# A decoder trunk of two layers: earlier first gathers, VectorE operations that signal themselves, and phase ends copied out by halves

## The chip, the cores and the metric

One core of a Trainium2 chip runs the whole program. The metric is the device time of one execution in microseconds.

## The reference

The input x is 256 positions of 1024 numbers in float32. Two residual layers follow; each is a mixer and then a mixture of single-neuron experts. The mixer of layer 0 is pooling with dilated attention, the one of layer 1 a Mamba-2 scan. The expert part, which moves most of the bytes, is this for each block of 128 positions:

```python
def block(xb):
    q = jnp.einsum('nd,de->ne', xb, w_q).astype(jnp.float32).reshape(n, PEER_HEADS, 2, PEER_HALF)
    s = jnp.einsum('nhie,ike->nhik', q, keys)
    top_s, top_i = lax.top_k(s, PEER_TOPK)
    ...
    best_s, best_pos = lax.top_k(cand_s, PEER_TOPK)
    idx = jnp.take_along_axis(cand_i, best_pos, axis=-1)
    gate = jax.nn.softmax(best_s, axis=-1)
    u = expert_u[idx]
    act = jax.nn.gelu(jnp.einsum('nhkd,nd->nhk', u, xb, preferred_element_type=jnp.float32), approximate=False)
    coef = (gate * act).astype(xb.dtype)
    return jnp.einsum('nhk,nhkd->nd', coef, expert_v[idx])
```

There are 8 heads, and each picks 16 of 16384 experts for every position. So every position fetches 128 rows of u and 128 rows of v for each layer.

## The kernel before

The program has four **phases**: layer 0 with block 0, layer 0 with block 1, layer 1 with block 0, layer 1 with block 1. A phase has 128 **slots**, 16 for each head. One slot is one gather of 128 partitions by 2048 numbers (u and v of one expert for each position), 1 MB. `gather` on GpSimd (POOL, L500) issues them into `ring`, which has 12 places, in pairs: a pair goes out once TensorE has summed the pair that used the same places (`pairs_summed0` and `pairs_summed1`). The first gather of each head also waits for that head's expert numbers (`idx_ready`). The ring's places serve as weight buffers at first (`staged`): gathers 0 to 11 also wait for `staged_free`, which PE tells when it has used a weight chunk. Gathers 8 and 9 wait for the query chunk of heads 4 and 5, gathers 10 and 11 for the one of heads 6 and 7.

For each slot VectorE (DVE) takes a dot product (`dot`, L1584). For each pair ScalarE (ACT) takes the gelu (L1141), DVE multiplies by the gates (`coefficients`, L1592), ACT makes two diagonal matrices (L1148), and PE adds both rows into four accumulator banks `acc` in PSUM (`sum_pair`, L928, 16 records for a pair). Even slots are summed in one half of the partitions of a bank, odd slots in the other half, crossed over.

Beside this stream, the mixer and the queries of the next phase run in small pieces. Each engine's program is written by generators (`Side`), and tables of numbers (`KNOTS`, `TOPS_DUE`, `ROUTE_DUE`) say before which slot each piece is put. `queries` on PE makes a head's query (L610), ACT copies it (L990), PE multiplies it with the keys (L890), ACT copies the scores, DVE picks the 16 largest of both halves (`tops`, L1483 to L1487). `route` then works in three parts on DVE: part 0 adds up the candidates and picks the 16 best, part 1 (`expert_numbers`, L1533 to L1552) computes the expert numbers, part 2 the gates. `queries` also makes the norm's gain on all partitions with 8 products (16 records, L899), behind the first head's keys. DVE needs it for `hn` later on.

In the very first phase nothing runs beside: the mixer of block 0 and the queries of all heads come ahead of the first slots (`T_EARLY`, `T_ROUTED`).

At a **phase end** ACT copies the odd sums from `acc` to `odd_sums` (`copy_odd`, L1160). DVE waits for all of it and adds the even sums from `acc` on top, into `h` (`read_acc`, L1604, behind slot 2). PE waits for that, then puts the new phase's own stream into `acc` (`take_stream`, L912, 4 products, 8 records), and only then sums the new phase's first pair. Part 1 of `route` for head 1 stands right behind `read_acc` on DVE.

At the **start** SP issues x, then the constants (312 KB), then the first weight chunk in two halves of 1024 KB, then more chunks. PE begins with transposes of x, for which it needs the identity, a part of the constants.

Many steps end with `lane.tell(name)`: DVE waits for its own last operation and then adds to a semaphore with an instruction of its own. `lane(instruction, name)` lets the operation itself add to that semaphore.

## Time and profile before

| | us |
|---|---|
| median of 3 runs | 1625.21 (1623.24 to 1626.09) |
| the profiled execution | 1629.12 |
| its span, first to last instruction | 1627.3 |
| PE busy | 1202.7 (74%) |
| DVE busy | 1171.0 (72%) |
| POOL busy | 600.7 (37%) |
| ACT busy | 527.0 (32%) |
| bytes moved | 665.05 MB, mean 409 GB/s |

The page cuts the span in 40 slices and gives for each the GB/s that the 16 DMA engines moved. The view by windows gives the same for stretches of one's own choice. In the timeline, a bracket behind an instruction tells how long its engine stood idle before it, and what ended that. "DVEq" and "ACTq" are the instruction queues of DVE and ACT, where semaphores are added to.

### The profile page before, as it was taken

How to read it: one execution, taken by the hardware profiler on the slowest of the kernel's cores; microseconds unless marked ns; L12 is line 12 of the kernel's file. 1: busy time of each engine (PE TensorE's matmuls, PEld its weight loads, DVE VectorE, ACT ScalarE, POOL GpSimd, SP SyncE). 2: the span in 40 equal slices, each digit the busy share in tenths (PEclk: the TensorE clock that was granted, in tenths of full speed). 3: DMA queues.
4: the chain of work that ended last, by engine and by line, in shares of the span. 5: the costliest groups of instructions: out<-in, count | busy, mean ns of one | idle time of the engine just before them, and what ended most of it. 6: DMA issues, size and time to landing. Idle time of an engine off the chain costs nothing.

```text
span 1627.3 us, 21833 instructions
## 1 busy us (share of the span) xinstructions
PE 1202.7 (74%) x7488; PEld 591.0 (36%) x7488; DVE 1171.0 (72%) x3339; ACT 527.0 (32%) x1231; POOL 600.7 (37%) x542
## 2 busy tenths in 40 slices
PE   8876786868748887978687788799697855555565
PEld 3661232225415663533264355444234611111111
DVE  4479768668768687786677866788956886666665
ACT  0222143222224564642132355455311232222221
POOL 1034433533334244233333323441433345444442
PEclk9998897989879998998898799999798988777767
DMA  9879999999999999999999999999999989999997
GB/s 380 339 297 412 423 421 421 422 421 421 421 417 415 423 425 420 420 423 422 422 422 422 384 424 424 421 421 417 395 414 424 416 354 421 422 421 421 421 421 315
DMA packets 84079, 665.05 MB, mean 409 GB/s; under 512 B 9376, under 2 KB 9392, under 8 KB 11008
## 3 DMA queue, kind: packets, MB, share of 16 engines
q0 software_dynamic: 74752, 540.13, 80.3%
q1 hardware_dynamic: 9216, 123.53, 18.0%
q8 instruction: 59, 0.97, 0.2%
q14 instruction: 52, 0.43, 0.1%
HBM read 662.57 MB, written 1.05 MB: 408 GB/s over the span
## 4 chain that ended last, share of the span: by engine, by line
DMA 29%; PE 29%; DVE 26%; ACT 7%; issue 7%; POOL 2%; another core or an unknown queue 0%; DVEq 0%; POOLq 0%; ACTq 0%; SPq 0%
DMA ring<-in_experts,idx 28%; PE acc L928 11%; DVE ring L1584 9%; PE act_bank L610 7%; PE dve_bank L596 6%; DVE h L1390 2%; DVE onehot L1219 2%; DVE scratch L1219 2%; POOL ring L500 2%; ACT diag L1148 1%; ACT L990 1%; ACT h L1070 1%; PE act_bank L596 1%; ACT scratch L990 1%; PE act_bank L890 1%
## 5 line engine op out<-in xcount | busy, mean ns | idle before, releaser
L500 POOL DMA_INDIRECT ring<-in_experts,idx x510 | 573.5, 1125 | 947.6 <-PE acc L928 732.0
L928 PE MATMUL acc<-ring,diag 64*64 64x512 f32 x4080 | 608.2, 720 | 315.8 <-ACT diag L1148 307.9
L1584 DVE CUSTOM_DVE_ANT_0 ring<-ring,hn 128x1024 f32<-128x1024 f32 x512 | 620.7, 1224 | 220.1 <-DMA ring<-in_experts,idx 197.1
L928 PEld LDWEIGHTS acc<-ring,diag 64*64 64x64 f32 x4080 | 155.1, 153 | 665.2 <-ACT diag L1148 427.2
L1141 ACT ACTIVATE acts<-dots 128x2 f32<-128x2 f32 x256 | 52.1, 203 | 674.6 <-DVE dots L1584 642.2
L610 PE MATMUL act_bank<-hnT,wbuf 128*128 128x128 f32 x1728 | 218.0, 284 | 23.3 <-ACT h L1070 19.5
L1148 ACT ACTIVATE diag<-cst,coefs 128x64 f32<-128x64 f32 x512 | 150.3, 340 | 252.1 <-DVE coefs L1592 215.4
L610 PEld LDWEIGHTS act_bank<-hnT,wbuf 128*128 128x128 f32 x1728 | 205.2, 197 | 70.1 <-issue 63.0
L990 ACT ACT_TABLE_LOAD x80 | 102.6, 1283 | 19.4 <-DMA rowc<-in_rows 17.0
L1592 DVE TENSOR_TENSOR coefs<-acts,gate 128x2 f32<-128x2 f32 x256 | 42.7, 167 | 79.5 <-ACT acts L1141 64.7
L1141 ACT ACT_TABLE_LOAD x68 | 87.2, 1283 | 6.2 <-DVE dots L1584 0.3
L1390 DVE SCALAR_TENSOR_TENSOR h<-scratch,colc,h 128x128 f32<-128x128 f32 x192 | 64.7, 406 | 0.8
L596 PE MATMUL dve_bank<-wbuf,scratch 128*128 128x512 f32 x128 | 63.2, 627 | 0.3 <-PE dve_bank L596 0.2
L990 ACT ACTIVATE scratch<-act_bank 128x512 f32<-128x512 f32 (+3 forms) x73 | 35.3, 484 | 74.9 <-PE act_bank L610 51.7
L837 PE MATMUL act_bank<-wbuf,hnT 128*128 128x512 f32 x128 | 59.0, 598 | 0.0
L890 PE MATMUL act_bank<-keysT,scratch 128*128 128x128 f32 x128 | 23.3, 307 | 34.6 <-issue 19.7
L1584 DVE DVE_READ_ACCUMULATOR2_ANT dots<- 128x1 f32 x512 | 42.2, 82 | 0.0
L596 PEld LDWEIGHTS dve_bank<-wbuf,scratch 128*128 128x128 f32 x128 | 23.4, 198 | 42.6 <-issue 42.6
L596 PE MATMUL dve_bank<-wbuf,hnT 128*128 128x512 f32 x64 | 33.9, 675 | 5.2 <-DVE hnT L1219 3.3
L890 PEld LDWEIGHTS act_bank<-keysT,scratch 128*128 128x128 f32 x128 | 17.7, 200 | 45.1 <-issue 45.1
L837 PEld LDWEIGHTS act_bank<-wbuf,hnT 128*128 128x128 f32 x128 | 23.3, 190 | 24.7 <-issue 24.3
L1483 DVE MAX8 top_s<-scores 128x8 f32<-128x128 f32 x64 | 15.5, 284 | 22.8 <-ACTq L361 22.5
(173 smaller groups left out, 1024.8 us busy)
## 6 DMA issues: line engine op xcount, KB each, us to landing
wbuf<-in_weights SPq DMA_DIRECT2D x48, 2048.0 KB
ring<-in_weights SPq DMA_DIRECT2D x7, 2048.0 KB, 19.4
ring<-in_experts,idx POOLq DMA_INDIRECT x510
kept<-in_weights SPq DMA_DIRECT2D x2, 2048.0 KB, 21.8
wbuf<-in_weights SPq DMA_DIRECT2D x2, 1024.0 KB, 7.0
scratch<-in_bias POOLq DMA_DIRECT2D x1, 1024.0 KB, 12.0
scratch<-in_bands POOLq DMA_DIRECT2D x1, 768.0 KB, 13.3
h<-in_x SPq DMA_DIRECT2D x1, 512.0 KB, 3.7
```

The source lines that it names most:

```text
L500: pool.indirect_dma_start(ring[:, n % RING], None, io[f"experts{layer}"], bass.IndirectOffsetOnAxis(idx[:, at:at + 1], 0),).then_inc(sem(f ...
L596: ins = pe.matmul(out[:, 0:cols], lhsT[:, k], w[:, k], start=first and k == tiles[0], stop=last and k == tiles[-1])
L610: ins = pe.matmul(out[:, n * P:(n + 1) * P], w[:, k, j * P:(j + 1) * P], hnT[:, k], start=k == 0, stop=k == KD - 1)
L837: ins = pe.matmul(out_z, hnT[:, k], w[:, k], start=k == 0, stop=k == KD - 1)
L890: ins = pe.matmul(out[:, i * NK:(i + 1) * NK], qT[:, 2 * hd + i], keysT[:, layer, i], start=True, stop=True)
L928: last[rows] = pe.matmul(acc[rows][half][home:home + HALF_P], diag[part, n % DIAGS], ring[part, slot, D + half * CW:D + (half + 1) * CW], ...
L990: lane(act.activation(out, in_, func, **more), name)
L1141: act.activation(acts[:, cols], dots[:, cols], ACT.Gelu).then_inc(sem("gelu_done"), 1)
L1148: ins = act.activation(diag[:, (q * GROUP + s) % DIAGS], folded, ACT.Copy, scale=coefs[:, q * GROUP + s:q * GROUP + s + 1])
L1219: lane(dve.tensor_tensor(out, in0, in1, op), name)
L1390: done = lane.start(dve.scalar_tensor_tensor(out, tiles[:, j, tap:tap + P], taps[:, t, tap:tap + 1], out, ALU.mult, ALU.add))
L1584: dve.tensor_tensor_reduce(out=ring[:, slot, 0:D], in0=ring[:, slot, 0:D], in1=hn[:, phase % NBLK], scale=1.0, scalar=0.0, op0=ALU.mult, o ...
```

## The change

- **Start.** The constants are sorted anew, and SP first issues only 160 of their 624 columns (identity and the mixer's gains, 80 KB), then x, then the first half chunk as two quarters of 512 KB, the second half, and the other 464 columns. PE waits for a quarter, and for the second quarter behind its second product.
- **First head.** In the first phase, head 0 has its expert numbers in two halves: as soon as the 8 best are picked, DVE computes their 8 numbers and signals `first_idx_ready`, on which gather 0 waits. The other 8 follow. ACT takes the exponential of head 0 behind the second head's scores instead of the third's. Heads 2 and later have their tops one piece later.
- **Gain.** The 8 products of the gain stand ahead of the first head's query in all four phases.
- **Signals.** Some 20 places with `lane.tell` on DVE now let the last operation signal (those of `mixer0`, `mixer1`, `prepare`, `tops`, `route`).
- **Phase ends.** DVE copies the even sums from `acc` into `h` (`copy_even`) without waiting for ACT; both signal each half (512 columns). PE starts the first pair's sums in a half when it is copied out. `take_stream` stands behind the fourth pair, and adds to what is there. DVE adds the odd sums behind slot 3 (`add_odd`). Part 1 of head 1 goes out at slot 4 or later.

The core of the diff (most places of the signals are left out):

```diff
-EARLY_HEADS, ROUTED_HEADS = 6, 3
+EARLY_HEADS, ROUTED_HEADS = 6, 2
...
+TAKEN_AT = 3 * GROUP + 1
...
+ROUTE_FROM = 4
...
-            ROUTE_DUE.append(max(_due, _part) if _head else _due)
-TOPS_FIRST = 3
-TOPS_DUE = [-3, -2, -2, 0, 1, 1, 3, 5]
+            if _head == 1:
+                _due = max(_due, _phase * SLOTS + ROUTE_FROM + _part - 1) if _phase and _part else max(_due, _part)
+            ROUTE_DUE.append(_due)
+TOPS_FIRST = 2
+TOPS_DUE = [-3, -2, 0, 1, 2, 3, 4, 5]
...
-C_ID, C_TRI, C_STRI, C_IOTA = 0, P, 2 * P, 3 * P
+C_ID, C_GAIN = 0, P
+C_FFN = C_GAIN + DEPTH * KD
+C_FIRST = C_TRI = C_FFN + DEPTH * KD
+C_STRI = C_TRI + P
+C_IOTA = C_STRI + P
...
-C_GAIN = C_FOLD + HALF_P
-C_FFN = C_GAIN + DEPTH * KD
-C_ROWS = C_FFN + DEPTH * KD
+C_ROWS = C_FOLD + HALF_P
...
+            sp.dma_start(cst[:, 0:C_FIRST], io["consts"][:, 0:C_FIRST]).then_inc(sem("first_consts_loaded"), 16)
...
-            sp.dma_start(cst, io["consts"]).then_inc(sem("consts_loaded"), 16)
...
-                            sp.dma_start(flat[:, 0:CH // 2], w[:, 0:CH // 2]).then_inc(sem("half_chunk_in"), 16)
+                            quarter, half = slice(0, CH // 4), slice(CH // 4, CH // 2)
+                            sp.dma_start(flat[:, quarter], w[:, quarter]).then_inc(sem("quarter_chunk_in"), 16)
+                            sp.dma_start(flat[:, half], w[:, half]).then_inc(sem("half_chunk_in"), 16)
...
+                            sp.dma_start(cst[:, C_FIRST:], io["consts"][:, C_FIRST:]).then_inc(sem("consts_loaded"), 16)
...
-                if n % TOPK == 0:
+                if n == 0:
+                    pool.wait_ge(sem("first_idx_ready"), 1)
+                elif n == TOPK // 2 or n % TOPK == 0:
...
                 if chunks[0] == 1:
-                    pe.wait_ge(sem("half_chunk_in"), 16)
+                    pe.wait_ge(sem("quarter_chunk_in"), 16)
                     return wbuf[:, 0]
...
                     score(groups[1])
+                def second_quarter():
+                    if b == 0:
+                        pe.wait_ge(sem("half_chunk_in"), 16)
...
-                                                  halfway={0: other_half, 3: first_scores}.get(c))
+                                                  between={0: {1: second_quarter, 3: other_half},
+                                                           3: {3: first_scores}}.get(c, {}))
...
+                pe.wait_ge(sem("consts_loaded"), 16)
+                for half in range(2):
+                    out = fill("dve")
+                    for j in range(4):
+                        row = layer * KD + 4 * half + j
+                        ins = pe.matmul(out[:, j * P:(j + 1) * P], ident[:, row:row + 1].to_broadcast([P, P]),
+                                        gain_rows, start=True, stop=True)
+                    ins.then_inc(sem("dve_full"), 1)
...
-                    if hd == 0:
-                        yield at + 3
-                        for half in range(2):
-                            out = fill("dve")
-                            for j in range(4):
-                                row = layer * KD + 4 * half + j
-                                ins = pe.matmul(out[:, j * P:(j + 1) * P], ident[:, row:row + 1].to_broadcast([P, P]),
-                                                gain_rows, start=True, stop=True)
-                            ins.then_inc(sem("dve_full"), 1)
...
                                         h[part, phase % NBLK, half * CW:(half + 1) * CW],
-                                        start=True, stop=False, skip_group_check=True)
+                                        start=False, stop=False, skip_group_check=True)
                     ins.then_inc(sem("stream_taken"), 1)
...
+                    if start and g:
+                        pe.wait_ge(sem("even_copied"), 2 * (g // STEPS - 1) + half + 1)
+                        pe.wait_ge(sem("odd_copied"), 2 * (g // STEPS - 1) + half + 1)
...
-                                                   start=start and odd == 1, stop=stop, skip_group_check=True)
+                                                   start=start, stop=stop, skip_group_check=True)
...
-                    if n == GROUP:
-                        if phase:
-                            pe.wait_ge(sem("acc_read"), phase)
-                            pe.wait_ge(sem("odd_copied"), phase)
-                        take_stream(phase)
...
+                    if n == TAKEN_AT:
+                        take_stream(phase)
...
-            pe.wait_ge(sem("consts_loaded"), 16)
+            pe.wait_ge(sem("first_consts_loaded"), 16)
...
-                lane.after(started)
-                lane.tell("odd_copied")
+                    lane.after(started)
+                    lane.tell("odd_copied")
...
-                        started[n] = lane.start(step(*row))
+                        last = step == steps[-1] and n == len(rows) - 1
+                        started[n] = lane.start(ops[step](*row), name if last else None)
...
-                lane(dve.tensor_copy(norm_root, stat[:, 32:33]))
-                lane.tell("root_ready")
+                lane(dve.tensor_copy(norm_root, stat[:, 32:33]), "root_ready")
...
-                                 top_i[:, hd, i * TOPK:(i + 1) * TOPK]) for i in range(2)))
-                        lane.tell("scores_taken")
+                                 top_i[:, hd, i * TOPK:(i + 1) * TOPK]) for i in range(2)), name="scores_taken")
...
-                    top16((cand, best, best_pos))
-                def expert_numbers(hd):
-                    row, place, beyond = (pos_f[:, n * TOPK:(n + 1) * TOPK] for n in range(3))
+                def expert_numbers(hd, lo, hi, name):
+                    picks = slice(lo, hi)
+                    row, place, beyond = (pos_f[:, n * TOPK:(n + 1) * TOPK][:, picks] for n in range(3))
...
-                    started = [lane.start(dve.tensor_scalar(pos_hi, best_pos, 4, None, ALU.logical_shift_right)),
-                               lane.start(dve.tensor_scalar(pos_lo, best_pos, 15, None, ALU.bitwise_and)),
-                               lane.start(dve.tensor_copy(top_if, top_i[:, hd]))]
+                    started = [lane.start(dve.tensor_scalar(pos_hi[:, picks], best_pos[:, picks], 4, None,
+                                                            ALU.logical_shift_right)),
+                               lane.start(dve.tensor_scalar(pos_lo[:, picks], best_pos[:, picks], 15, None,
+                                                            ALU.bitwise_and))]
+                    if lo == 0:
+                        started.append(lane.start(dve.tensor_copy(top_if, top_i[:, hd])))
...
-                    lane.start(dve.tensor_copy(row, pos_hi))
+                    lane.start(dve.tensor_copy(row, pos_hi[:, picks]))
...
-                    lane(dve.tensor_copy(place, pos_lo))
+                    lane(dve.tensor_copy(place, pos_lo[:, picks]))
...
-                    hot = onehot.rearrange("p (i s a) -> p i s a", i=2, s=TOPK)
-                    flat = onehot.rearrange("p (n a) -> p n a", a=TOPK)
-                    tt(flat, pos_f[:, 0:2 * TOPK].unsqueeze(2).to_broadcast([P, 2 * TOPK, TOPK]),
-                       iota16.unsqueeze(1).to_broadcast([P, 2 * TOPK, TOPK]), ALU.is_equal)
-                    tt(hot, hot, key.unsqueeze(2).to_broadcast([P, 2, TOPK, TOPK]))
-                    lane(dve.reduce_sum(picked, flat, AX))
-                    stt(row, picked[:, 0:TOPK], float(NK), picked[:, TOPK:], ALU.mult, ALU.add)
-                    at = b * SLOTS + hd * TOPK
-                    lane(dve.tensor_copy(idx[:, at:at + TOPK], row))
-                    lane.tell("idx_ready")
+                    n = hi - lo
+                    hot = onehot.rearrange("p (i s a) -> p i s a", i=2, s=TOPK)[:, :, picks]
+                    found = picked.rearrange("p (i s) -> p i s", i=2)[:, :, picks]
+                    both = pos_f[:, 0:2 * TOPK].rearrange("p (i s) -> p i s", i=2)[:, :, picks]
+                    tt(hot, both.unsqueeze(3).to_broadcast([P, 2, n, TOPK]),
+                       iota16.unsqueeze(1).unsqueeze(1).to_broadcast([P, 2, n, TOPK]), ALU.is_equal)
+                    tt(hot, hot, key.unsqueeze(2).to_broadcast([P, 2, n, TOPK]))
+                    lane(dve.reduce_sum(found, hot, AX))
+                    stt(row, found[:, 0], float(NK), found[:, 1], ALU.mult, ALU.add)
+                    at = b * SLOTS + hd * TOPK + lo
+                    lane(dve.tensor_copy(idx[:, at:at + n], row), name)
...
-                        lane(dve.tensor_copy(last_idx, place[:, 0:2 * GROUP]))
-                        lane.tell("last_idx_ready")
+                        lane(dve.tensor_copy(last_idx, place[:, 0:2 * GROUP]), "last_idx_ready")
...
-                ts(expd, best, best[:, 0:1], None, ALU.subtract)
-                lane.tell("best_ready")
+                start = 0
+                if layer == b == hd == 0:
+                    top16((cand, best, best_pos), steps=range(2))
+                    start = TOPK // 2
+                    expert_numbers(hd, 0, start, "first_idx_ready")
+                    top16((cand, best, best_pos), steps=range(2, 5))
+                else:
+                    top16((cand, best, best_pos))
+                ts(expd, best, best[:, 0:1], None, ALU.subtract, name="best_ready")
...
-                expert_numbers(hd)
+                expert_numbers(hd, start, TOPK, "idx_ready")
...
-            def read_acc(phase):
+            def copy_even(phase):
...
-                lane.need("odd_copied")
...
-                        started = lane.start(dve.tensor_tensor(h[part, phase % NBLK, cols], odd_sums[part, cols],
-                                                               acc[rows][half][part], ALU.add))
-                lane.after(started)
-                lane.tell("acc_read")
+                        started = lane.start(dve.tensor_copy(h[part, phase % NBLK, cols], acc[rows][half][part]))
+                    lane.after(started)
+                    lane.tell("even_copied")
+            def add_odd(phase):
+                for half in range(2):
+                    lane.need("odd_copied")
+                tt(h[:, phase % NBLK], h[:, phase % NBLK], odd_sums, ALU.add)
...
-                        read_acc(phase - 1)
+                        copy_even(phase - 1)
+                    if n == GROUP + 1 and phase:
+                        add_odd(phase - 1)
...
             tops_side.upto(0)
+            dve.wait_ge(sem("consts_loaded"), 16)
             routes.upto(ROUTE_PARTS - 1)
```

**PE, first phase, from the transposes of h behind the mixer to the second head's query** (L610 is a query, L890 the keys, L899 the gain). Before:

```order
L618 MATMUL act_bank<-cst,h 128x128 x8
L610 MATMUL act_bank<-hnT,ring 128x128 x16
L890 MATMUL act_bank<-keysT,scratch 128x128 x2
L899 MATMUL dve_bank<-cst 128x128 x8
L610 MATMUL act_bank<-hnT,ring 128x128 x16
```

Now, where L621 is a query, L915 the keys and L893 the gain:

```order
L629 MATMUL act_bank<-cst,h 128x128 x8
L893 MATMUL dve_bank<-cst 128x128 x8
L621 MATMUL act_bank<-hnT,ring 128x128 x16
L915 MATMUL act_bank<-keysT,scratch 128x128 x2
L621 MATMUL act_bank<-hnT,ring 128x128 x16
```

The gain moved ahead of the first query, into the place where PE waits for ACT's copies of `hnT`.

**DVE, first phase, the first head from the places of its 8 best** (`best_pos`, first row). Before:

```order
L1484 MAX_INDEX best_pos<-best,cand 128x8
L1485 MATCH_REPLACE cand<-best,cand 128x136
L1486 MAX best<-cand 128x8
L1487 MAX_INDEX best_pos<-best,cand 128x8
L1223 TENSOR_SCALAR expd<-best 128x16
L1533 TENSOR_SCALAR pos_hi<-best_pos 128x16
L1534 TENSOR_SCALAR pos_lo<-best_pos 128x16
L1535 CAST top_if<-top_i 128x32
L1537 CAST pos_f<-pos_hi 128x16
L1539 CAST pos_f<-pos_lo 128x16
L1226 SCALAR_TENSOR_TENSOR pos_f<-pos_f 128x16
L1542 TENSOR_TENSOR pos_f<-pos_f 128x16
```

Now, from the ninth row behind that same `MAX_INDEX` (L1492) on:

```order
L1235 TENSOR_TENSOR onehot<-pos_f,cst 128x2x128
L1235 TENSOR_TENSOR onehot<-onehot,top_if 128x2x128
L1561 TENSOR_REDUCE picked<-onehot 128x2x8
L1242 SCALAR_TENSOR_TENSOR pos_f<-picked 128x8
L1564 CAST idx<-pos_f 128x8
L1493 MATCH_REPLACE cand<-best,cand 128x136
L1494 MAX best<-cand 128x8
L1495 MAX_INDEX best_pos<-best,cand 128x8
L1239 TENSOR_SCALAR expd<-best 128x16
L1540 TENSOR_SCALAR pos_hi<-best_pos 128x8
```

Eight expert numbers (`idx`) are now written ahead of the second half of the picking, on arrays half as long.

**DVE, end of the first phase, from the second slot of the new phase on** ("ISA ring,dots" and "ISA dots" are one dot product). Before:

```order
L1592 TENSOR_TENSOR coefs<-acts,gate 128x2
L1584 ISA ring,dots<-ring,hn 128x1024
L1584 ISA dots 128x1
L1604 TENSOR_TENSOR h<-scratch,acc 64x512 x4
L1533 TENSOR_SCALAR pos_hi<-best_pos 128x16
L1534 TENSOR_SCALAR pos_lo<-best_pos 128x16
L1535 CAST top_if<-top_i 128x32
```

Now:

```order
L1609 TENSOR_TENSOR coefs<-acts,gate 128x2
L1601 ISA ring,dots<-ring,hn 128x1024
L1601 ISA dots 128x1
L1620 COPY h<-acc 64x512 x4
L1601 ISA ring,dots<-ring,hn 128x1024
L1601 ISA dots 128x1
L1235 TENSOR_TENSOR h<-h,scratch 128x1024
L1609 TENSOR_TENSOR coefs<-acts,gate 128x2
L1601 ISA ring,dots<-ring,hn 128x1024
L1601 ISA dots 128x1
```

Four copies took the place of four additions, one addition of 1024 columns was added behind the next dot product, and the 13 operations of part 1 of head 1 went behind slot 4.

## Rows read from the trace of the kernel before

**Rows 1.** The page's GB/s in 40 slices, and its group of the dot products

```profile
GB/s 380 339 297 412 423 421 421 422 421 421 421 417 415 423 425 420 420 423 422 422 422 422 384 424 424 421 421 417 395 414 424 416 354 421 422 421 421 421 421 315
...
L1584 DVE CUSTOM_DVE_ANT_0 ring<-ring,hn 128x1024 f32<-128x1024 f32 x512 | 620.7, 1224 | 220.1 <-DMA ring<-in_experts,idx 197.1
```

**Rows 2.** By windows: stretch, length, busy time of PE, PEld, DVE, ACT, POOL

```profile
core 0: us, PE busy (x) PEld busy (x) DVE busy (x) ACT busy (x) POOL busy (x), PEclk, DMA share, GB/s
70.00:80.00 10.00, 9.12 (x72) 8.77 (x71) 4.63 (x27) 1.11 (x3) 0.00 (x0) 0.91 0.30 128
80.00:90.00 10.00, 8.51 (x72) 8.19 (x72) 6.67 (x27) 1.67 (x5) 3.86 (x4) 1.00 0.33 111
110.00:120.00 10.00, 7.34 (x53) 4.12 (x51) 7.81 (x35) 4.37 (x8) 2.82 (x4) 1.00 0.56 204
900.00:930.00 30.00, 23.56 (x160) 10.33 (x156) 25.40 (x65) 9.20 (x24) 12.78 (x12) 0.81 0.95 371
1320.00:1330.00 10.00, 7.29 (x60) 2.00 (x55) 9.06 (x23) 2.37 (x9) 5.02 (x5) 0.95 0.48 177
```

**Rows 3.** Timeline of the first 10 us, PE and DVE: start, us, instruction

```profile
5.27 1.97 PE L618 MATMUL dve_bank<-cst,h 128*128 128x128 f32 x8 [5.27 <-DMA cst<-in_consts]
8.79 9.57 PE L596 MATMUL dve_bank<-wbuf,hnT 128*128 128x512 f32 x16 [1.55 <-DMA wbuf<-in_weights]
...
6.52 1.51 DVE L1219 TENSOR_TENSOR hnT<-dve_bank,cst 128x512 f32<-128x512 f32 x2 [0.68 <-PE dve_bank L618]
```

**Rows 4.** The chain of work that ended last, until 120 us: start, us, what

```profile
18.65 7.12 PE dve_bank L596 x16
...
74.35 1.79 PE dve_bank L899 x16
76.14 3.59 PE act_bank L610 x32
...
89.26 2.96 another core or an unknown queue
...
110.93 1.87 PE acc L912 x8
```

**Rows 5.** Timeline of PE, the first head's query

```profile
67.61 5.47 PE L610 MATMUL act_bank<-hnT,ring 128*128 128x128 f32 x32 [1.84 <-ACT hnT L1110]
```

**Rows 6.** Timeline of DVE, the first head's numbers

```profile
78.49 0.29 DVE L1484 FIND_INDEX8 best_pos<-best,cand 128x8 uint32<-128x136 f32 x1
...
79.96 0.23 DVE L1223 TENSOR_SCALAR expd<-best 128x16 f32<-128x16 f32 x1
80.34 0.18 DVE L1533 TENSOR_SCALAR pos_hi<-best_pos 128x16 uint32<-128x16 uint32 x1
...
81.37 0.69 DVE L1219 TENSOR_TENSOR onehot<-pos_f,cst 128x512 f32<-128x512 f32 x1
...
83.75 0.17 DVE L1552 CAST idx<-pos_f 128x16 uint32<-128x16 f32 x1
```

**Rows 7.** Timeline of POOL, gathers 0 and 10

```profile
84.95 1.01 POOL L500 DMA_INDIRECT ring<-in_experts,idx  x1 [29.58 <-DVEq L361]
...
115.88 0.94 POOL L500 DMA_INDIRECT ring<-in_experts,idx  x1 [9.41 <-PEq L586]
```

**Rows 8.** Groups by form, DVE: two that stand nearest to new ones

```profile
L1219 DVE TENSOR_TENSOR scratch<-scratch,hn 128x256 f32<-128x256 f32 x8 | 3.4, 425 | 0.3
...
L1219 DVE TENSOR_TENSOR h<-scratch 128x1024 f32<-128x1024 f32 x1 | 1.2, 1226 | 0.0
```

**Rows 9.** Timeline, ends of phase 2 (1312) and of phase 1 (896)

```profile
1311.94 2.44 ACT L1160 ACTIVATE scratch<-acc 64x512 f32<-64x512 f32 x4
1314.55 2.83 DVE L1604 TENSOR_TENSOR h<-scratch,acc 64x512 f32<-64x512 f32 x4 [2.12 <-ACTq L361]
...
1319.28 1.12 PE L928 MATMUL acc<-ring,diag 64*64 64x512 f32 x2
...
1323.76 1.25 POOL L500 DMA_INDIRECT ring<-in_experts,idx  x1 [11.99 <-PE acc L928]
...
896.20 2.83 DVE L1604 TENSOR_TENSOR h<-scratch,acc 64x512 f32<-64x512 f32 x4 [1.22 <-ACTq L361]
```

More of the change, by code:

```diff
@@ L591, in chunk_used, with row_products @@
                 chunk_free()
-            def row_products(out, lhsT, w, first=True, last=True, cols=CW, tick=None, halfway=None, tiles=range(KD)):
+            def row_products(out, lhsT, w, first=True, last=True, cols=CW, tick=None, between={}, tiles=range(KD)):
                 for k in tiles:
@@ L1477, in mixer1, with top16 @@
                     lane.tell("h_ready")
-            def top16(*rows):
-                steps = [
+            def top16(*rows, steps=range(5), name=None):
+                ops = [
                     lambda src, values, places: dve.max(values[:, 0:8], src),
```

52 lines of the change are left out of this document (22 added, 30 removed).

## The prediction

> **What bounds the kernel now.** I read the page's GB/s by slices first. Almost everywhere the transfers run at 421 to 424 GB/s, and DVE's dot products, the nearest engine work, stood idle 220.1 us, of it 197.1 for gathers [rows 1]. So the stream of gathers sets the pace, and a microsecond is won only where the stream stands still: 665.05 MB at 422 GB/s are 1576 us of a span of 1627.3, and the other 51 us are holes. The view by windows prices each hole as (422 − its rate) / 422 × its length [rows 2]: 70 to 80 us 7.0 us, 80 to 90 us 7.4, 110 to 120 us 5.2, the end of phase 1 (900 to 930) 3.6, the end of phase 2 (1320 to 1330) 5.8. The end of phase 0 shows only in the slices of 417 and 415, (5 + 7) / 422 × 40.7 = 1.2 us [rows 1]. The change works on all of these. The chain of waits then tells what ends each hole: at the start PE's products, the first query, the first head's numbers; at a phase end the copies out of `acc` and the first pair's sum behind them.
>
> **Start.** PE waits for the constants until 5.27, and before the first chunk's products 1.55 us for the half chunk; their other operand `hnT` is done at 6.52 + 1.51 = 8.03 [rows 3]. Now 232 KB of constants and 512 KB of weights come behind what PE needs first. That is 0.75 MB, 1.8 us at 422 GB/s. But `hnT` allows only 8.79 − 8.03 = 0.76, and it can itself move by some tenths since its constants are 80 KB instead of 312. Against this, x is now the second DMA in SP's queue and one more 512 KB DMA is issued. I also see PE at its lower clock level in this stretch: 16 products take 9.57 us, the next 16 take 7.12 [rows 3, 4]; the 2.45 could come back in part if PE starts otherwise. I take **0.6 us**, the near end; bounds −0.3 (one issue of x late) and +2.2 (all of it).
>
> **Signals.** Behind `expd` (79.96 + 0.23 = 80.19) the next operation starts at 80.34, 0.15 us later, where neighbours without a `tell` follow in some hundredths [rows 6]. So a `tell` costs DVE about 0.1. Four or five lie on the way to the first gather: **0.4 us**. The hundred others lie beside DVE's waits and are worth nothing.
>
> **Gain ahead of the first query.** PE idles 1.84 us before that query, waiting for ACT's copies of `hnT`, and then needs 5.47 us for 32 records; the next 32 take 3.59, and the granted clock of that stretch is 0.91 against 1.00 after it [rows 2, 4, 5]. The 16 records of the gain take 1.79 us [rows 4] and fill just this idle time. If the clock then stays at its full level, the query takes 3.59: **1.9 us** for head 0 (bounds 0 and 1.9). For PE's later queries the 1.79 that stood between heads 0 and 1 vanish too.
>
> **Half numbers.** Before: 8 places at 78.49 + 0.29 = 78.78, `idx` at 83.75 + 0.17 = 83.92 [rows 6], gather 0 at 84.95 [rows 7]. From `pos_hi` on the chain takes 83.92 − 80.34 = 3.58. In halves, the second picking, `expd` and the `tell` fall out of the way (80.34 − 78.78 = 1.56), and the three operations on `onehot` have 256 columns: 0.43 for 0.69, 3 × 0.26 = 0.8 [rows 6, 8]. Together **2.4 us**. Head 0 pays for them with 12 more small operations, about 2 us of DVE, behind the signal. The second half is needed by gather 8 only, some ten microseconds later at 1.24 us a gather. POOL has nothing else queued there.
>
> Gather 0 thus goes out 0.6 + 0.4 + 1.9 + 2.4 = 5.3 us earlier, at about **79.6**.
>
> **The second hole.** Gather 10 waits 9.41 us for PE, to 115.88 [rows 7]: PE must be through with the last query's weights. On this path DVE's numbers don't lie. What does: start 0.6, signals 0.4, clock 1.9, the gain's 1.8, and `take_stream`, 1.87 us at 110.93 [rows 4], which goes behind the fourth pair. Sum 6.6, gather 10 at about 109.3. What lies behind it moves by that, so **the head is worth 6.6 us**, of which 5.3 came already by gather 0. Bounds: 3.8 (start −0.3, clock 0) and 8.2 (start 2.2).
>
> **Phase ends.** At the end of phase 2 ACT copies to 1314.38, DVE has waited 2.12 us for it, adds for 2.83 to 1317.38; then come `take_stream` and at 1319.28 the first pair; the gather goes out at 1323.76 after 11.99 us idle of POOL [rows 9]. Now DVE starts at once, at 1314.55 − 2.12 = 1312.43, and PE can sum half 0 when 2 of the 4 copies are made. At 0.7 us each (2.83 / 4) that is 1313.9, and 1315.2 for both halves. From the first pair's start to the gather it took 1323.76 − 1319.28 = 4.5: begun at 1313.9 it gives 1318.4, and I take 1318.5, **5.2 us earlier**, half 1 being ready while half 0 is summed. Of the hole's 5.8 I take 5.4 (bounds 4 and 5.8); its rest is the time that the row of gathers needs to build up. The end of phase 1 is another matter: DVE waited only 1.22 [rows 9], and the new addition of 1024 columns gives 1.23 back before the second pair. The hole there (3.6) comes from DVE's other work in slots 2 to 6, which now lies a little later. I take 0.6 (bounds 0 and 3.6), and for phase 0's end 0.5 (0 and 1.2). Together **6.5 us**, bounds 4 and 10.6.
>
> `take_stream` behind the fourth pair costs PE the same as before; `sum_pair` carries two waits more, which are met. Three additions of 1.23 us [rows 8] and the 12 small operations are about 5 us more of DVE: hidden by its waits for gathers, 197.1 us [rows 1]; without that cover they would cost those 5 us.
>
> The new addition reads two SBUF arrays beside POOL's gather issues, and POOL's issue at a phase end already takes 1.25 us against 0.94 at gather 10 [rows 7, 9]. If one blocks the other for its whole length, each of three additions costs 1.2 us: 3.7 less. The Trainium skill (SBUF — State Buffer, Who interferes with whom) says that a DVE instruction with two SBUF inputs and a GpSimd one that uses SBUF share a port pair under an exclusive lock. By it the gain would be 9.4 us, not 13.1. I don't take this off, since twelve gathers are in flight and the row shows 0.3 us at most.
>
> **Sum.** 6.6 + 6.5 = 13.1 us. The profiled execution took 1629.12, so 1616.0 for it; it was 3.9 above the median, 1625.21, and against that the forecast is **1612**.
>
> **Rivals.** (A) As forecast, both bounds sum to 7.8 and 18.8; the likely part is 9 to 17 us, 1608 to 1616. Chance 0.55. (B) More: the start brings its 2.2 and the ends of phases 0 and 1 close as well; 17 to 20, 1605 to 1608. For it the queue behind `hnT`; against it that DVE, not the copies, is late at those ends. 0.15. (C) Less: the clock stays low in the first query (−1.9), and the stall of 2.96 us at 89.26, which the chain gives to an unknown queue just as the first gathers land [rows 4], comes 5 us sooner and hits PE's queries or DVE's numbers of the second half; with the lock above 13.1 − 1.9 − 3 − 2 = 6, so 1616 to 1620. For it: the stall is in the trace, and it has no cause in the program. 0.20. (D) No gain: the earlier gathers only wait elsewhere, since from gather 12 on places come free by DVE's dots, PE's pairs and their diagonals; the head's 6.6 is given back where DVE is 7.8 of 10 us busy and catches up [rows 2], and the ends keep about 2: 1623. Against it the 421 GB/s just behind. 0.07. (E) Slower, by one mechanism: DVE is the bound wherever the stream falls behind. Then the holes are DVE's backlog, no release helps, and the 5 us of new DVE work at the three ends and the first head come on top: 1630. It decides from the point where DVE's share right behind a hole is at 10 of 10; it is 9.06 of 10 in 1320 to 1330 [rows 2]. Against it: in that window POOL had stood 11.99 us for PE's sum, not for a dot. 0.03. That the change doesn't do what it says has no room of its own: the order shows each move.
>
> **Numbers.** 0.2% is 3.3 us, about what a measurement of this kernel can tell from no change: faster is below 1622.0, slower above 1628.5. A, B, C and a part of D lie below: 0.91 faster, 0.06 same, 0.03 slower. The range takes A, most of B and all of C: 1604 to 1620.
>
> **What would show it.** Right: the constants' wait ends before 5.2; the first query takes about 3.6 with next to no idle before it; the first `idx` is written near 78.6 and gather 0 is issued near 79.6; gather 10 near 109; POOL's idle at the end of phase 2 falls from 12 to about 7, and the window 1320 to 1330 is back at about 420 GB/s. Four copies of about 0.7 and an addition of 1.2 stand at each phase end. Wrong in its steps: a first query still at 5.5 (clock); gather 0 at 79.6 but gather 10 still beyond 113 (another thing than PE's order releases it); gathers earlier but a new hole between 90 and 110 us (case C or D); DVE without idle time and additions longer than 1.3 us at the ends (lock, case E).

## The result, and the profile after

| | before | changed |
|---|---|---|
| median of 20 runs | 1625.22 us (1623.24 to 1627.21) | 1627.29 us (1625.16 to 1628.93) |
| ratio, 95% interval | | 1.0013 [1.0007, 1.0019] |
| profiled execution | 1629.12 | 1627.79 |
| its span | 1627.3 | 1625.8 |

The change costs some 2 us. I had forecast 1612 within 1604 to 1620, and the measured time lies above all of that. Most single steps did happen, though. Timelines of the changed kernel, of PE, DVE and POOL:

```profile
5.40 1.94 PE L629 MATMUL dve_bank<-cst,h 128*128 128x128 f32 x8 [5.40 <-DMA h<-in_x]
8.19 8.90 PE L607 MATMUL dve_bank<-wbuf,hnT 128*128 128x512 f32 x16 [0.85 <-DVE hnT L1235]
...
66.47 3.84 PE L621 MATMUL act_bank<-hnT,ring 128*128 128x128 f32 x32
...
78.56 0.17 DVE L1564 CAST idx<-pos_f 128x8 uint32<-128x8 f32 x1
...
79.70 1.02 POOL L511 DMA_INDIRECT ring<-in_experts,idx  x1 [25.57 <-DVE idx L1564]
...
105.70 1.32 POOL L511 DMA_INDIRECT ring<-in_experts,idx  x1 [7.57 <-PEq L597]
...
120.22 0.94 POOL L511 DMA_INDIRECT ring<-in_experts,idx  x1 [9.16 <-PE acc L947]
```

The first query takes 3.84 us and not 5.47 [rows 5], the first half of the numbers is there at 78.56, gather 0 goes out at 79.70 for 84.95 and gather 10 at 105.70 for 115.88 [rows 7]. But then POOL stands 9.16 us for a pair's sum, until gather 14 at 120.22. The view by windows (columns as in [rows 2]):

```profile
80.00:90.00 10.00, 8.49 (x72) 8.19 (x72) 9.47 (x42) 1.93 (x5) 7.87 (x8) 1.00 0.86 322
110.00:120.00 10.00, 3.69 (x16) 0.80 (x16) 6.09 (x30) 4.25 (x8) 0.94 (x1) 0.54 0.91 352
120.00:130.00 10.00, 6.35 (x36) 2.25 (x38) 9.32 (x32) 2.17 (x9) 3.26 (x4) 0.61 0.60 214
900.00:930.00 30.00, 21.58 (x155) 10.18 (x151) 24.77 (x75) 10.08 (x24) 12.72 (x13) 0.84 0.95 371
1300.00:1320.00 20.00, 9.90 (x52) 2.42 (x56) 18.77 (x55) 7.94 (x18) 9.17 (x8) 0.72 0.99 392
1320.00:1330.00 10.00, 9.68 (x72) 3.98 (x64) 7.21 (x16) 2.38 (x9) 4.55 (x5) 0.87 0.99 376
```

Against [rows 2] two things are to be seen. The hole of 204 GB/s at 110 to 120 is not gone, it is now one of 214 at 120 to 130. And the hole of 177 at 1320 to 1330 is nearly closed (376), yet the end did not come sooner. The page's GB/s by slices says the same:

```profile
GB/s 377 343 364 375 422 422 421 422 421 421 422 422 405 422 424 420 422 423 423 422 422 423 384 424 423 421 421 423 399 425 421 420 394 422 421 421 421 421 421 242
```

The last slice has 242 for 315 [rows 1]: most bytes are through some microseconds earlier, and the kernel waits at its end for something else. The same at the end of the changed kernel, by windows:

```profile
1600.00:1605.00 5.00, 1.95 (x16) 0.51 (x16) 2.62 (x5) 0.83 (x4) 0.00 (x0) 1.00 1.01 409
1605.00:1610.00 5.00, 3.01 (x16) 0.62 (x16) 2.63 (x5) 0.80 (x4) 0.00 (x0) 0.58 0.41 166
1610.00:1615.00 5.00, 3.75 (x20) 0.85 (x20) 3.36 (x6) 0.79 (x3) 0.00 (x0) 0.50 0.07 27
```

From 1610 to 1615 the DMA share is 0.07 and the rate 27 GB/s: a sixteenth of 1.01 and of 421 is 0.063 and 26. One of 16 DMA engines is at work, and the dot products wait for it:

```profile
1607.71 1.22 DVE L1601 CUSTOM_DVE_ANT_0 ring<-ring,hn 128x1024 f32<-128x1024 f32 x1 [1.23 <-DMA ring<-in_experts,idx]
...
1612.60 1.23 DVE L1601 CUSTOM_DVE_ANT_0 ring<-ring,hn 128x1024 f32<-128x1024 f32 x1 [1.25 <-DMA ring<-in_experts,idx]
```

The trace also has the time of each of the 16 additions to a gather's semaphore. The Trainium skill (DMA: Bandwidth & Descriptors, Why a DMA increments its semaphore by 16 and not by 1) says that each engine posts its own and that they finish independently. The trace agrees: in the changed kernel they spread over 0.5 to 1.8 us at 125 to 140 us and over 11.0 us at the end, where 15 of the 16 lie within 1.5 us.

**Theory 1** (slow engine): one DMA engine falls behind the other 15, and the end hangs on it. It catches up while the stream stands still. So a hole is free up to its lag, and closing one gains nothing. **Theory 2** (order): at the head DVE's and ACT's fixed order sets when places come free, and the tops, put one piece later, spoil it. The rival to both: the new parts themselves cost what they save.

### The profile page after: what moved, and what is told of

Same layout as the page of the kernel before. It is cut to its first block, busy times and chain, and to the rows that moved or that the text cites. A ratio compares the mean times of both kernels' runs of the same rounds, so it can differ in the third digit from the quotient of the medians.

```text
span 1625.8 us, 21843 instructions
## 1 busy us (share of the span) xinstructions
PE 1202.8 (74%) x7488; PEld 589.3 (36%) x7488; DVE 1174.8 (72%) x3354; ACT 527.1 (32%) x1231; POOL 600.7 (37%) x542
## 4 chain that ended last, share of the span: by engine, by line
DMA 30%; DVE 27%; PE 27%; ACT 8%; issue 6%; POOL 1%; SPq 0%; ACTq 0%; POOLq 0%; DVEq 0%
DMA ring<-in_experts,idx 30%; PE acc L947 12%; DVE ring L1601 9%; PE act_bank L621 5%; PE dve_bank L607 4%; DVE h L1399 2%; DVE onehot L1235 2%; ACT L1006 2%; ACT diag L1165 2%; PE act_bank L854 1%; ACT h L1086 1%; PE act_bank L607 1%; DVE scratch L1235 1%; POOL ring L511 1%; ACT scratch L1006 1%
## 5 line engine op out<-in xcount | busy, mean ns | idle before, releaser
L947 PE MATMUL acc<-ring,diag 64*64 64x512 f32 x4080 | 616.2, 730 | 348.8 <-ACT diag L1165 329.2
L621 PE MATMUL act_bank<-hnT,wbuf 128*128 128x128 f32 x1728 | 215.0, 282 | 20.7 <-ACT h L1086 19.3
L621 PEld LDWEIGHTS act_bank<-hnT,wbuf 128*128 128x128 f32 x1728 | 202.2, 195 | 68.4 <-issue 66.2
L915 PE MATMUL act_bank<-keysT,scratch 128*128 128x128 f32 x128 | 22.8, 302 | 29.8 <-issue 18.4
L915 PEld LDWEIGHTS act_bank<-keysT,scratch 128*128 128x128 f32 x128 | 17.2, 195 | 41.5 <-issue 41.5
L1491 DVE MAX8 top_s<-scores 128x8 f32<-128x128 f32 x64 | 15.5, 283 | 20.5 <-ACTq L367 20.4
```

The source lines that it names most:

```text
L621: ins = pe.matmul(out[:, n * P:(n + 1) * P], w[:, k, j * P:(j + 1) * P], hnT[:, k], start=k == 0, stop=k == KD - 1)
L947: last[rows] = pe.matmul(acc[rows][half][home:home + HALF_P], diag[part, n % DIAGS], ring[part, slot, D + half * CW:D + (half + 1) * CW], ...
```

## The experiments

Each was timed beside the kernel before, apart from the first. Where a time is set against one that was not timed together with it, the kernel before stood within 1624.9 to 1626.2 beside all of them, so such a difference is good to about 1 us. In the expectations "tops" are the steps L1491 to L1495 that pick the 16 largest scores, and "dot n" is DVE's dot product for slot n in the first phase. One slip of mine stands in them: what the expectations of tops_back, whole_numbers, gain_back and tops_later call dot 8, at 122.9 us in the changed kernel, is dot 6 (and the dots 4 and 6 of tops_later are dots 2 and 4); the text here counts rightly.

**The kernel before again.**

> The kernel before once more, for a second profile: the first one (1629.12 us) lies above all 20 of its timed runs (1623.2 to 1627.2). Slow-engine theory: the transfers of one gather are done by 16 DMA engines, and one of them falls behind the others; in the first profile the 16 landings of a gather spread over 8 us shortly ahead of the end of phase 2, and over 1.6 us behind the hole of 1320 to 1330, in which the late engine caught up. The second profile shows the same: a spread of 7 to 13 us at 1290, under 3 us at 1350, and a hole of 177 GB/s or so in 1320 to 1330. Rival (the spread in the first profile was chance, all engines alike): a spread under 3 us throughout. Time 1624 to 1627 by both.

1624.67 us. The spread was 7.9 us at 1290 and 1.6 at 1350, as theory 1 has it. But the hole was not one of 177 GB/s in 1320 to 1330, as expected; it lay across both windows:

```profile
1300.00:1320.00 20.00, 9.06 (x48) 2.60 (x52) 15.90 (x51) 7.32 (x15) 6.14 (x5) 0.74 0.81 337
1320.00:1330.00 10.00, 7.05 (x60) 1.69 (x52) 9.09 (x22) 2.76 (x11) 7.69 (x7) 1.00 0.88 338
```

That is 85/422 × 20 + 84/422 × 10 = 6.0 us, and the late engine lost none of it. Two gathers on either side of the hole have half of their landings 9.7 us apart (at 1315.1 and 1324.8), but their last ones, at 1323.0 and 1325.5, only 2.5 us apart, as in the full stream. More important is the head. Here gather 0 goes out at 83.89 and gather 10 at 110.47, 5.4 us earlier than in the trace on which I had forecast:

```profile
83.89 1.01 POOL L500 DMA_INDIRECT ring<-in_experts,idx  x1 [29.58 <-DVEq L361]
...
110.47 0.94 POOL L500 DMA_INDIRECT ring<-in_experts,idx  x1 [8.86 <-PEq L586]
```

Beside this one, the changed kernel leads by 5.1 us at dot 0 (87.98 for 93.07) and is 2.4 behind at dot 6 (122.90 for 120.54). It is 2.8 behind at dot 62 and 1.1 at the last dot of the phase.

**Phase ends taken back, and phase ends alone.** In `ends_back` the diff's parts on the phase ends are undone in the changed kernel; in `ends_only` they alone are made in the kernel before. The core of the latter's edit (the halves, the copies and part 1 of head 1 are left out):

```diff
-                    if n == GROUP:
-                        if phase:
-                            pe.wait_ge(sem("acc_read"), phase)
-                            pe.wait_ge(sem("odd_copied"), phase)
-                        take_stream(phase)
...
+                    if n == TAKEN_AT:
+                        take_stream(phase)
...
+                    if n == GROUP + 1 and phase:
+                        add_odd(phase - 1)
```

> The changed kernel (1627.3 us) with the phase ends of before: read_acc waits for all odd copies and adds, take_stream ahead of the first pair, part 1 of head 1 not held back. Slow-engine theory: the hole at the end of phase 2 lets the late engine catch up and costs it nothing, so the time stays within 1.5 us of the changed kernel, 1625.8 to 1628.8, though the slice at 1320 falls back below 250 GB/s; the landings of the last gathers then spread over less than 5 us instead of 11. Rival (the new phase ends do save their 4 to 6 us, and the head loses more than it gains): 1631 to 1633.

> The kernel before (1625.2 us) with the new phase ends alone (even copies without waiting, halves, take_stream behind the fourth pair, add_odd, part 1 of head 1 from slot 4). Slow-engine theory: the hole at 1320 to 1330 closes (over 350 GB/s for 177), the landings of the last gathers spread over 8 to 12 us, and the time stays within 1.5 us of before: 1623.7 to 1626.7. Rival (all engines alike, the hole was worth its 5.8 us): 1619 to 1621. Third (the new ends cost what the changed kernel lost): 1627 to 1629.

`ends_back`: 1626.68, 0.6 below the changed kernel (ratio to before 1.0004 [0.9995, 1.0013], where the changed kernel has 1.0013). `ends_only`: 1625.77 beside 1625.92 for before, ratio 1.0003 [0.9994, 1.0012]. Both times are theory 1's. The sizes in the traces are not quite: in `ends_back` the spread at the end fell to 8.5 and not under 5, and its hole was one of 335 and 363 GB/s, not under 250. In `ends_only` the hole closed and the spread at the end is 8.0:

```profile
1320.00:1330.00 10.00, 8.26 (x48) 3.07 (x52) 9.08 (x22) 2.58 (x10) 3.00 (x3) 0.66 0.95 369
```

**A hole made on purpose.** In `gather` (changed kernel, and later the kernel before):

```diff
+DRAINED = 448
...
+                if n == DRAINED:
+                    pool.wait_ge(sem(f"rows_in{(n - 1) % RING}"), 16 * ((n - 1) // RING + 1))
                 at = n % (NBLK * SLOTS)
```

> The changed kernel with one wait more: GpSimd issues gather 448 (mid phase 3) only when gather 447 has landed whole, so the stream runs dry once. Slow-engine theory: 15 engines stand idle for 11 to 14 us, the late one (8 to 11 us behind there) only for 2 to 4 us, and the time grows by only 2 to 4.5 us, to 1629.5 to 1632; behind the drain the landings of a gather spread over less than 3 us. Rival (all engines alike): what the stream loses by the GB/s in the windows, 11 to 14 us, is lost in full, 1638 to 1641.

> The kernel before with the same one wait of GpSimd ahead of gather 448 as in drain. There the landings of a gather spread over some 3 us, not 10. By the windows the stream should lose 5 to 7 us instead of 12.7. Slow-engine theory: the price is the restart of the late engine alone, as in drain (4.6 us there): 3 to 5 us more than before. Rival (a hole costs its lost bytes): 5 to 7 us, and less than half of what it cost in drain, which has been told wrong there already.

The window of `drain`, then that of `drain_before`:

```profile
1440.00:1480.00 40.00, 22.55 (x112) 5.16 (x112) 24.29 (x62) 8.12 (x24) 14.47 (x14) 0.67 0.70 287
```

```profile
1440.00:1480.00 40.00, 20.06 (x112) 4.80 (x112) 24.55 (x63) 8.44 (x25) 18.59 (x16) 0.74 0.87 356
```

| | bytes lost, as time | lag there before it | price |
|---|---|---|---|
| `drain` | 134/421 × 40 = 12.7 us | 10.6 us | 1631.87 − 1627.29 = 4.6 us |
| `drain_before` | 66/422 × 40 = 6.3 us | 3.2 us | 1629.36 − 1625.29 = 4.1 us |

Twice the loss, the same price. (4.6 is 0.1 us above the 2 to 4.5 that I had given; `drain` and the changed kernel were not timed together, and by what each has above the kernel before, 5.95 and 2.07, it is 3.9.) The landings say what the price is: the time for which the late engine itself stands still. The last landings on either side of the stop lie at 1457.3 and 1463.9 in `drain` and at 1453.2 and 1460.0 in `drain_before`, 4.1 and 4.3 us more than the usual 2.5. The spread of a gather's 16 landings over time, worked out from the semaphore's records, in us (of a gather near the time given; at other times, behind a weight chunk above all, it is wider for a few gathers):

```
                 1290   1350   1430   end (without the last one)
before_again      7.9    1.6    2.7    4.6 (2.7)
changed          10.3    8.8    9.9   11.0 (1.5)
ends_back         9.7    4.6    5.6    8.5 (2.7)
ends_only         8.2    5.1    6.1    8.0 (3.5)
drain            10.4    9.6   10.6    2.3 (1.8)
drain_before      7.9    1.8    3.2    2.9 (2.2)
tops_again       11.3   10.1   11.1   12.8 (2.9)
both_again        9.8    5.7    6.7    8.6 (2.0)
```

The end shows the bound as well. In the 17 traces of this case the span ends 9.5 to 11.4 us behind the last landing of the last gather, but anywhere from 11.5 to 20.9 us behind half of its landings.

**The tops in their old places.** In the changed kernel; `tops_later` does the reverse in the kernel before, and nothing else:

```diff
-TOPS_FIRST = 2
-TOPS_DUE = [-3, -2, 0, 1, 2, 3, 4, 5]
+TOPS_FIRST = 3
+TOPS_DUE = [-3, -2, -2, 0, 1, 1, 3, 5]
```

> The changed kernel (1627.3 us) with the places of the tops in the first phase as before (TOPS_FIRST 3, TOPS_DUE -3 -2 -2 0 1 1 3 5): one edit of two lines. Order theory: with the tops one piece later, ScalarE waits for them in its fixed order (5.70 us at 111.05 in the changed kernel), the gelu of the second pair stands behind, and DVE idles 2.27 and 3.87 us before its coefficients, where the kernel before has no idle from 87 to 120 us. Put back, these 6 us go, dot 8 starts at 117.5 to 118.5 instead of 122.9, and as behind it everything keeps its pace, the time is 1622 to 1624. Rival (the second hole is set by the release of places by TensorE, or by the late DMA engine): within 1 us of the changed kernel, 1626.3 to 1628.3.

> The kernel before (1626 us) with nothing but the changed kernel's places of the tops (TOPS_FIRST 2, TOPS_DUE -3 -2 0 1 2 3 4 5). Order theory: ScalarE waits for the tops ahead of the gelu of the second pair and DVE idles some 4 to 6 us ahead of dots 4 and 6 where it had none; dot 8 starts 3 to 5 us later and the time is 1629 to 1631. Rival (the later tops only hurt together with the earlier gathers of the changed kernel): within 1 us of before.

`tops_back`: 1621.14, ratio to before 0.9968 [0.9957, 0.998], 6.2 us below the changed kernel and 0.9 below the range expected; dot 6 starts at 118.85. `tops_later`: 1630.76 beside 1624.89, ratio 1.003 [1.0019, 1.0042], so 5 to 6 us above. The reason stands in ACT's and DVE's timelines. Changed kernel, between dots 1 and 4:

```profile
97.89 0.47 ACT L1006 ACTIVATE scores<-act_bank,stat 128x256 f32<-128x256 f32 x1 [2.68 <-DVE top_i L1495]
...
99.77 0.20 ACT L1158 ACTIVATE acts<-dots 128x2 f32<-128x2 f32 x1
100.08 0.16 DVE L1609 TENSOR_TENSOR coefs<-acts,gate 128x2 f32<-128x2 f32 x1 [2.27 <-ACT acts L1158]
...
111.05 0.47 ACT L1006 ACTIVATE scores<-act_bank,stat 128x256 f32<-128x256 f32 x1 [5.70 <-DVE top_i L1495]
...
114.53 0.20 ACT L1158 ACTIVATE acts<-dots 128x2 f32<-128x2 f32 x1
114.84 0.16 DVE L1609 TENSOR_TENSOR coefs<-acts,gate 128x2 f32<-128x2 f32 x1 [3.87 <-ACT acts L1158]
```

The copy of a head's scores waits for the tops that free its buffer, since there are two. ACT takes its work in order, so the pair's gelu waits behind it, and DVE, which would do the next tops, waits for the gelu. With the tops in the old places (`tops_again`) there is no idle time before the same two rows:

```profile
103.70 0.16 DVE L1609 TENSOR_TENSOR coefs<-acts,gate 128x2 f32<-128x2 f32 x1
...
112.34 0.16 DVE L1609 TENSOR_TENSOR coefs<-acts,gate 128x2 f32<-128x2 f32 x1
```

`tops_later` shows both waits in the kernel before, 2.26 and 3.86 us, and dot 6 at 127.0 for 120.5, 6.5 us later where I had expected 3 to 5.

**Needless work for DVE.** Four copies of `hn` onto itself in the kernel before, behind dots 2 to 5 or behind dots 42 to 45:

```diff
+BUSY = (2, 3, 4, 5)
...
                     dot(phase, g, n % BODY)
+                    if phase == 0 and n in BUSY:
+                        lane(dve.tensor_copy(hn[:, 0], hn[:, 0]))
```

> The kernel before (1625.9 us on this chip) with 4 needless copies of 1024 columns on DVE in place (hn onto itself, 1.2 us each or somewhat less), one behind each of dots 2 to 5 of the first phase: 4 to 4.9 us of DVE work. DVE theory (behind the first gathers DVE's queue of tops, numbers and dots sets when places come free): the time grows by nearly all of it, 3.5 to 5 us. Rival (the stream or the late DMA engine is the bound there): by less than 1 us.

> The same 4 copies behind dots 42 to 45 of the first phase, at about 210 to 225 us, where DVE waits for gathers. Both theories: less than 0.8 us, unless DVE's work anywhere costs time, then 3.5 to 5 us.

A copy took 0.69 us, not 1.2, so 2.8 us in all. Early, dot 6 came 3.3 us later than with the late ones (124.4 for 121.1), 0.4 of it from the start. The times were 1627.67 and 1626.28 beside 1626.17: 1.5 and 0.1 us. The first lies between the two expectations, 3.5 to 5 us and under 1. So DVE's work ahead of slot 6 moves the stream there by its whole length, and about half of that is left at the end; the interval of the first, [0.9998, 1.0016], just holds no effect too. The same work at dots 42 to 45, where DVE waits for gathers, cost nothing that the runs can tell.

**Head 0's numbers in one piece**, on top of `tops_back`:

```diff
-                if layer == b == hd == 0:
+                if False:
...
-                if n == 0:
-                    pool.wait_ge(sem("first_idx_ready"), 1)
-                elif n == TOPK // 2 or n % TOPK == 0:
+                if n % TOPK == 0:
```

> As tops_back, and head 0's numbers in one piece of 16 again (no first_idx_ready). Order theory: gather 0 goes out 2.4 us later, at about 82, but DVE, which has no idle behind it until dot 8, is rid of 12 small operations (some 2 us less 0.8 for the shorter arrays of each half, so 1 to 2 us): dot 8 starts 1 to 2 us earlier than in tops_back and the time is 1620.5 to 1623, 1 to 2 us below tops_back. Rival (what counts is when the stream starts): 1.5 to 2.5 us above tops_back.

A miss of both expectations. Dot 6 does start 4.1 us earlier than in `tops_back` (114.7 for 118.8), more than I had said, of which 1.8 us were there at 64 us already. But the lead is down to 0.9 by slot 61 (267.0 for 267.9), at slot 383 it is 2.2 us behind (1292.1 for 1290.0), and the time is 1624.82 beside 1621.14, 3.7 us **above**. The landings explain it in part at most: at 320 to 326 us they spread over 5.2 us there and 3.4 in `tops_back`. What takes the lead back, no run shows.

**Gain and start taken back**, each on top of `tops_back`, with `both_back` (old phase ends on top of `tops_back`) timed together with them:

> tops_back (1621.1 us) with the 8 products of the gain behind the first head's keys again. The first query should take 5.4 us at the lower clock level instead of 3.8, with 1.8 us idle of TensorE before it, and gather 0 goes out some 1.7 us later. DVE theory: DVE's queue behind head 0's numbers, full until dot 8, moves by as much: 1 to 2 us more, 1622.1 to 1623.1. Rival (the head's numbers are no bound any more): within 0.5 us; third, my sum for TensorE's path in the prediction (clock 1.9 and products 1.8): 3.7 us more.

> tops_back (1621.1 us) with the start of before: x, then all 312 KB of constants, then the first chunk in two halves. In the profiles TensorE's first products of the first chunk start at 8.33 to 8.79 us with the old start and at 8.19 to 8.72 with the new one, which waits for x 0.1 to 0.6 us longer. Expected by that: no difference, within 0.7 us. Rival (the prediction's term of 0.6 us, up to 2.2): 0.6 to 2.2 us more.

> tops_back (1621.1 us) with the phase ends of before as well, so that of the change the start, the half numbers, the gain and the signals are left. Slow-engine theory: the holes at the phase ends cost the late DMA engine nothing here either: within 1.5 us of tops_back, 1619.6 to 1622.6, the landings of the last gathers spread over 4 to 9 us instead of 13. Rival (with the head mended the new ends are worth their forecast 4 to 6 us): 1625 to 1627.

`gain_back`: 1623.04, `start_back`: 1621.81, `both_back`: 1621.55. The gain behind the keys costs 1.2 to 1.5 us against the other two, which differ from it in their start or their phase ends as well. Its first query shows what the prediction read from the clock:

```profile
67.03 5.46 PE L621 MATMUL act_bank<-hnT,ring 128*128 128x128 f32 x32 [1.91 <-ACT hnT L1128]
```

The start alone makes no difference that the runs can tell: `start_back` is 0.3 us above `both_back`, 0.7 above `tops_back`. But `tops_back` had stood at 0.9968 of before, and these three, timed apart from it, stand at 0.9991, 0.9981 and 0.9984. Two kernels were therefore timed again, together:

> tops_back once more (the changed kernel with the tops in their old places), to stand beside both_again on one chip. Order theory: 3.5 to 6 us below before, ratio 0.9963 to 0.9978.

> both_back once more (tops in their old places and the old phase ends). Slow-engine theory: within 1.5 us of tops_again. Rival (the new ends are worth something once the head is mended): 2 to 6 us above tops_again.

1621.13 (0.9976 [0.9967, 0.9985]) and 1621.69 (0.9979 [0.997, 0.9988]). The new phase ends are worth 0.6 us, less than the runs can tell from nothing. Yet the bytes are through much sooner with them, in `tops_again` by 1600:

```profile
1600.00:1605.00 5.00, 2.03 (x20) 0.63 (x16) 2.67 (x7) 0.79 (x3) 0.00 (x0) 0.95 0.09 36
1605.00:1610.00 5.00, 2.94 (x16) 0.55 (x12) 3.54 (x6) 0.79 (x3) 0.00 (x0) 0.50 0.06 26
```

Its last gather has half of its landings at 1597.5 and the last at 1608.7; `both_again` has 1602.6 and 1609.5. Five microseconds won for the median engine, 0.8 for the late one.

## Why the prediction was wrong

- **"A microsecond is won only where the stream stands still", each at full price.** This is the step of the prediction that failed for the phase ends. The rate of 16 engines together was taken for the bound, and their term, 6.5 us, is the holes at full price. The bound is the latest of them, and the trace before had it: the 16 landings of a gather were 7.8 us apart in it shortly ahead of the hole, and 1.7 behind it. The closing came true, though at less than the full rate: the windows 1300 to 1330 lose 2.5 us (30/422 × 20 + 46/422 × 10), where the last of them alone lost 5.8 before. The term of 6.5 us for the phase ends measured 0.0 (`ends_only`), −0.6 (against `ends_back`) and 0.6 (`both_again`).
- **"The head is worth 6.6 us".** I summed TensorE's path to gather 10, which came true (105.70 for a forecast 109.3; against the second profile of before it is 4.8 us of the 6.6), and took what lies behind it to move along. That step failed. Behind it the places come free by the sums of pairs 1 and 2, and these hang on DVE and ACT. In the second profile of the kernel before DVE never idles for more than 0.2 us at a time from 87 to 120 us, so that path was as tight as the one I followed. That was the mechanism of case D, priced at 0.07, and part of E.
- **The tops one piece later** stand in the description of the change, and the prediction put no price on them. This is the omission that turned the sign: 5 to 6 us by `tops_later`, 6.2 by `tops_back`.
- **Gather 0.** From the first query's start to gather 0 it takes 17.34 us in both profiles of before and 13.24 in the changed kernel: 4.1 us won, for 1.9 + 2.4 + 0.4 = 4.7 forecast. By the same count `gain_back` has 14.87 and `whole_numbers` 15.51, so the clock gave 1.6 and the half numbers 2.3, and 0.2 is left for the signals, which no run took back alone. That gather 0 went out at 79.70 for a forecast 79.6 is partly luck: the first query starts between 66.47 and 68.17 in traces of the same start, and `tops_back` has gather 0 at 81.41.
- **Start 0.6**: 0 within the runs. PE waits for x until 5.40 now, where it had waited for the constants until 5.27, and `hnT` ends the next wait. My own bound, 8.79 − 8.03, was nearly all run-to-run: the second profile of before has 8.33.
- **Gain 1.9**: mechanism right (3.84 us for the query with it, 5.46 without), size in the time 1.2 to 1.5. **Half numbers 2.4**: as forecast at gather 0, but 3.7 us in the time by `whole_numbers`, for a reason not found.
- **The port of DVE and GpSimd.** The new additions took 1.22 us each, not longer than [rows 8], and not taking off 3.7 us was right. But the lock was not tried by them: at each of the three phase ends the next gather's issue starts 0.6 us after the addition has ended (896.78 + 1.22 = 898.00, issue at 898.59). The section that the prediction cites from the Trainium skill (SBUF — State Buffer, Who interferes with whom) is also narrower than told there: it has such a DVE instruction contend with a GpSimd instruction that reads SBUF, not with one that only writes it. POOL's issues of 1.34 to 1.71 us, for 0.94, come later, beside other work, and the kernel before has one of 1.57 at 1306.25, without any new addition.
- **The trace.** One execution was the base, 3.9 us above the median. Its excess lay right in the holes that I priced: gather 10 at 115.88 for 110.47 in the second profile. The stall of 2.96 us at 89.26, on which rival C leaned, is a part of it: the chain of none of the other 16 traces has it, so it belongs to that execution and not to the kernel.

The sum as measured: the tops +5.9 us, all the rest −4.2 (`tops_again` beside before), together +1.7, for +2.1 seen. Taken back one by one, the rest comes to about 0.6 + 1.3 + 3.7 = 5.6, more than 4.2, so its parts do not simply add up. `tops_again`, the changed kernel with two lines put back, is the best version here: 4.2 us below before and 6 below the changed kernel.

## What to carry to other kernels

A rate that is the sum of many DMA engines hides the slowest. Before a hole in the stream is priced, look whether the landings of one transfer spread, and whether the spread shrinks in the hole: then the hole is partly free. In a fixed order on several engines, price each piece that changes place, most of all where an engine has no idle time around it; and take a second profile of the kernel before, when the first lies outside its timed runs.

## What the runs showed of the hardware

With up to 12 gathers in flight one DMA engine was 7.6 to 11.3 us behind the first in every trace by 1290 us, the other 15 within 0.9 to 3.7.

Part of how it falls behind can be read from the traces. Between 1345 and 1600 us the last of a gather's landings comes every 2.5 us, and four times after 3.4 instead: in the changed kernel with those at 1358.7, 1434.3, 1507.3 and 1580.3. Each time a packet of 8 KB of instructions had started 2.4 to 3.3 us before that landing (at 1356.0, 1431.9, 1504.3 and 1577.0; such a packet takes 0.3 us). The ten traces in which the lag is still over 4 us at 1350 and which were not stopped on purpose have 40 such steps, and each of the 40 has its packet, 2.1 to 3.3 us ahead. Three other packets of 8 KB in the same stretch (1409.8, 1466.5 and 1565.2 in the changed kernel) leave the late engine alone. The kernel's 59 packets of 16 KB of instructions take about 1.07 us each, and near them it is mostly another engine that falls back by about 1 us: in `tops_again` one of the other 15 does so near each of the seven such packets from 1350.3 to 1592.2. That the instruction packets cause the steps is argued from this coincidence; no run moved or removed one. Why 0.3 us of packet should cost 1 us, and which partitions the late engine serves, stays open.
